# A hybrid decoder step on one core: three gate projections of the first chunk are split, their second halves moved behind the second tile's mixing

## The reference, cut to what matters

```
h = rmsnorm(x)
u_s5, x_lru, y_lru, g_a, g_b = split(h @ w_in)         # 512, 512, 512, 1024, 1024 columns
a_out = s5_branch(u_s5)                                # diagonal state space, then a gated product (w_glu)
b_out = rglru_branch(x_lru, y_lru)                     # convolution, gated scan
merged = sigmoid(g_a) * (a_out @ w_proj_a) + sigmoid(g_b) * (b_out @ w_proj_b)
x = x + merged @ w_out
q = rmsnorm(x) @ w_q                                   # 8 heads, 2 x 128 columns each
x = x + peer(...)     # per token and head: the 16 best of 128 x 128 experts; each gives a row of u and one of v
y = rmsnorm(x)
```

## Time and profile before

| | us |
|---|---|
| median of 3 runs | 3078.5 |
| lowest, highest | 3077.85, 3082.4 |
| profiled execution, its own time | 3078.11 |
| its span in the trace | 3075.9 |
| first gather issued | 188.71 |
| gather 8 issued | 210.43 |

### The profile page before, as it was taken

How to read it: one execution, slowest core, us unless ns; L and a number is a source line. 1 busy time by engine, 2 the same in 40 slices (tenths; PEclk the granted TensorE clock), 3 DMA queues, 4 the chain that set the end, 5 groups by cost and what they waited for, 6 DMA issues and landing times.

```text
span 3075.9 us, 40789 instructions
## 1 busy us (share of the span) xinstructions
PE 2371.8 (77%) x14580; PEld 1201.6 (39%) x14580; DVE 2151.1 (70%) x5362; ACT 1001.8 (33%) x3275; POOL 1201.1 (39%) x1048
## 2 busy tenths in 40 slices
PE   9997768889877778888877768888987775555565
PEld 8864325555343334454333324445433331111111
DVE  7758887765579887665468987766558887554445
ACT  2224433422234332432234332432233433222223
POOL 0014443333334444333343443334344344445443
PEclk9998989999988888989988879999989897777778
DMA  4569999999999999999999999999999999999998
GB/s 154 205 244 394 420 421 420 415 410 414 419 420 419 420 418 405 421 413 420 420 418 416 420 421 407 420 392 420 419 418 421 405 420 420 421 420 421 416 421 336
DMA packets 177354, 1224.74 MB, mean 398 GB/s; under 512 B 22504, under 2 KB 22888, under 8 KB 31616
## 3 DMA queue, kind: packets, MB, share of 16 engines
q0 software_dynamic: 148608, 1082.20, 85.1%
q1 hardware_dynamic: 27040, 135.62, 11.1%
q10 hardware_dynamic: 1504, 4.33, 0.4%
HBM read 1217.55 MB, written 4.51 MB: 397 GB/s over the span
## 4 chain that ended last, share of the span: by engine, by line
DMA 43%; PE 29%; DVE 15%; ACT 4%; POOL 4%; issue 3%; ACTq 1%; DVEq 0%; POOLq 0%
DMA arena<-in_uv,arena 42%; PE psum L2128 12%; PE psum L2022 8%; DVE arena L1702 7%; POOL arena L749 4%; ACT arena L797 4%; PE psum L2172 3%; DVE arena L1200 3%; PE psum L2192 2%; DVE arena L1208 1%; DMA arena<-in_w_ab 1%; PE psum L2204 1%; PE psum L2037 1%; ACT L797 1%; PE psum L2061 1%
## 5 line engine op out<-in xcount | busy, mean ns | idle before, releaser
L749 POOL DMA_INDIRECT arena<-in_uv,arena x1032 | 1197.9, 1161 | 1848.1 <-PE psum L2128 1505.5
L1702 DVE CUSTOM_DVE_ANT_0 arena<-arena 128x1024 f32<-128x1024 f32 x1024 | 1246.9, 1225 | 787.1 <-DMA arena<-in_uv,arena 752.2
L2128 PE MATMUL psum<-arena 64*64 64x512 f32 x8184 | 1214.2, 717 | 652.6 <-ACT arena L797 597.9
L797 ACT ACTIVATE arena<-arena 128x1 f32<-128x1 f32 (+4 forms) x2746 | 726.9, 302 | 1827.6 <-DVE arena L1702 1685.3
L2128 PEld LDWEIGHTS psum<-arena 64*64 64x64 f32 x8184 | 302.5, 151 | 1374.0 <-ACT arena L797 885.1
L2022 PE MATMUL psum<-arena 128*128 128x256 f32 (+1 forms) x2656 | 637.9, 396 | 8.6 <-ACT arena L797 6.1
L2022 PEld LDWEIGHTS psum<-arena 128*128 128x128 f32 x2656 | 508.0, 196 | 193.5 <-issue 118.4
L1200 DVE TENSOR_TENSOR arena<-arena 128x256 f32<-128x256 f32 (+12 forms) x561 | 250.0, 472 | 12.1 <-issue 0.4
L797 ACT ACT_TABLE_LOAD x119 | 152.7, 1283 | 11.1 <-DVE arena L1200 7.0
L797 ACT ACTIVATE arena<-psum 128x256 f32<-128x256 f32 (+5 forms) x254 | 98.6, 403 | 159.5 <-PE psum L2022 108.0
L2172 PE MATMUL psum<-arena 128*128 128x128 f32 (+2 forms) x640 | 120.7, 346 | 9.5 <-DMA arena<-in_w_ab 7.3
(11 more groups left out here) (137 smaller groups left out, 1000.4 us busy)
## 6 DMA issues: line engine op xcount, KB each, us to landing
arena<-in_w_in SPq DMA_DIRECT2D x56, 1024.0 KB
arena<-in_w_q SPq DMA_DIRECT2D x34, 1024.0 KB
arena<-in_uv,arena POOLq DMA_INDIRECT x1032
arena<-in_w_ab SPq DMA_DIRECT2D x12, 1024.0 KB
arena<-in_w_out SPq DMA_DIRECT2D x11, 512.0 KB, 16.0
arena<-in_keys SPq DMA_DIRECT2D x17, 256.0 KB, 15.1
arena<-in_w_ab SPq DMA_DIRECT2D x8, 512.0 KB, 11.1
arena<-in_x_tok SPq DMA_DIRECT2D x8, 512.0 KB
```

The source lines that it names most:

```text
L749: pool.indirect_dma_start(uvring[:, r], None, i_["uv"], bass.IndirectOffsetOnAxis(column, 0)).then_inc(uv_in[r], 16)
L797: return nc.scalar.activation(out, in_, f, **kw)
L1702: V.tensor_tensor_reduce(out=u, in0=u, in1=hn[i // (SLOT // 2)], scale=1.0, scalar=0.0, op0=ALU.mult, op1=ALU.add, accum_out=dots_[:, b % ...
L2128: ins = mm(PV[o:o + HP, half], dg[r:r + HP, PAIR * (b % 2) + k], uvring[r:r + HP, place(c, i) % UV, at:at + 512], start=(i % (SLOT // 2) = ...
```

## The change

For the first chunk the projections of slots 25, 26 and 27 (`LATE`; `m` = 13, 14, 15) take columns 0 to 127 only, and so does their tanh. Their columns 128 to 255 are projected after the second tile's mixing and before `head(1)`, as three units of their own (`U_LATE`), with a tanh each on ScalarE. Since `hT[0]` must live until then, the second tile's mixing writes to `ga`. The columns of `w_in` for `g_b` are reordered on the host (`GB_OF`), so that the three late blocks are `m` = 3, 4, 5, which the second mixing takes last. The weights stay: block 25 gets a home in `hn[1]` and a load of its own, 26 and 27 remain in their place of the ring. All counts of `unit` and `evac` behind move by three.

```diff
-U_MIX0, U_OUT0, U_Q0, U_MIX1, U_Q01, U_OUT1, U_Q1, UNITS0 = 36, 44, 52, 54, 62, 64, 72, 88
-SLOTS0 = UNITS0 - 4
+U_MIX0, U_OUT0, U_Q0, U_MIX1, U_LATE, U_Q01, U_OUT1, U_Q1, UNITS0 = 36, 44, 52, 54, 62, 65, 67, 75, 91
+GB_OF = (0, 1, 2, 6, 7, 3, 4, 5)
+LATE, LATE_FROM = (25, 26, 27), 20
+SLOTS0 = UNITS0 - 4 - len(LATE)
...
-HOMES = RESIDENT + PARKED + GLU_W + tuple(MIX_W)
+HOMES = RESIDENT + PARKED + GLU_W + tuple(MIX_W) + (("w_in", LATE[0]),)
...
 def slot_unit(c, l):
-    return l if l < U_GATE else ga_unit(c, l - U_GATE) if l < TRUNK else l + (8 if c else 4)
+    if c == 0 and l in LATE:
+        return U_LATE + l - LATE[0]
+    if l < TRUNK:
+        return l if l < U_GATE else ga_unit(c, l - U_GATE)
+    return l + (8 if c else 4 if l < U_Q01 - 4 - len(LATE) else 4 + len(LATE))
...
# ScalarE, before the queries of head 1
+                        for j, l in enumerate(LATE):
+                            act.wait_ge(unit, U_LATE + j + 1)
+                            af(gb[:, GB_OF[l - LATE_FROM], P:C], PB[j % 2][:, 0:P], ACT.Tanh, scale=0.5).then_inc(evac, 1)
...
# VectorE, second mixing
+                    held = [GB_OF[l - LATE_FROM] for l in LATE]
+                    if m in held:
+                        dve.wait_ge(evac, U_MIX0 + 2 + held.index(m) + 1)
-                    mix(0, m, U_MIX1 + 4 * (i // 4) + 3, late, [...])
+                    mix(0, m, U_MIX1 + 4 * (i // 4) + 3, late, [...], ga)
...
# TensorE, behind the second mixing
                 pe.wait_ge(hn_ok, 1)
+                for j, l in enumerate(LATE):
+                    w = slot(0, l)
+                    if j >= 2:
+                        pe.wait_ge(evac, U_MIX0 + 2 + j - 1)
+                    for t in range(KT):
+                        ins = mm(PB[j % 2][:, 0:P], w[:, P * t:P * t + P], hT[0][:, t, late], start=(t == 0), stop=(t == KT - 1))
+                    ins.then_inc(unit, 1)
                 head(1, U_Q01)
...
-                    project(c, ga_unit(c, m), U_GATE + m, hT[c], KT, n)
+                    project(c, ga_unit(c, m), U_GATE + m, hT[c], KT, P if first and U_GATE + m in LATE else n)
```

More of the change, by code:

```diff
@@ L64 @@
 EVACS = 56
-U_MIX0, U_OUT0, U_Q0, U_MIX1, U_Q01, U_OUT1, U_Q1, UNITS0 = 36, 44, 52, 54, 62, 64, 72, 88
-SLOTS0 = UNITS0 - 4
+U_MIX0, U_OUT0, U_Q0, U_MIX1, U_LATE, U_Q01, U_OUT1, U_Q1, UNITS0 = 36, 44, 52, 54, 62, 65, 67, 75, 91
+GB_OF = (0, 1, 2, 6, 7, 3, 4, 5)
+LATE, LATE_FROM = (25, 26, 27), 20
+SLOTS0 = UNITS0 - 4 - len(LATE)
 TRUNK = 28
-EVACS0 = 56
+EVACS0 = 56 + len(LATE)
 LAST_FIRST = (6, 7, 0, 1, 2, 3, 4, 5)
@@ L469, in build @@
             + [rows_[:, GLU_AT + DB * k:GLU_AT + DB * k + DB] for k in range(QT)] \
-            + [rows_[:, MIX_AT + D * k:MIX_AT + D * k + D] for k in (LAST_FIRST.index(m) for m in range(KT))]
+            + [rows_[:, MIX_AT + D * k:MIX_AT + D * k + D] for k in (LAST_FIRST.index(m) for m in range(KT))] \
+            + [hn[1]]
         dg = R.take(2 * PAIR, HP)
@@ L1066, in mixing_gate @@
                     act.wait_ge(unit, units(c) + u + 1)
-                    dst = (ga if m < KT else gb)[:, m % KT, 0:n]
+                    w = P if first and U_GATE + m in LATE else n
+                    dst = ga[:, m, 0:w] if m < KT else gb[:, GB_OF[m - KT], 0:w]
                     if m == KT:
                         act.wait_ge(halo_ok, c + 2)
-                    af(dst, PB[u % 2][:, 0:n], ACT.Tanh, scale=0.5).then_inc(evac, 1)
+                    af(dst, PB[u % 2][:, 0:w], ACT.Tanh, scale=0.5).then_inc(evac, 1)
                 for q in range(QT):
@@ L1779, in sample_scale, with mix @@
                 stt(x_tok[0:NS, 1], x_tok[0:NS, 1], ss[0:NS, 1:2], nfs[0:NS], ALU.mult, ALU.mult).then_inc(yos_ok, 1)
-            def mix(c, m, u, cols, bank):
+            def mix(c, m, u, cols, bank, mixed):
                 dve.wait_ge(unit, u + 1)
@@ L1787, in mix @@
                 settled(stt(B2, B2, 1.0, bank[1][:, 0:n], ALU.add, ALU.mult))
-                stt(hT[c][:, m, cols], A, 0.5, B2, ALU.mult, ALU.add).then_inc(mix_ok, 1)
+                stt(mixed[:, m, cols], A, 0.5, B2, ALU.mult, ALU.add).then_inc(mix_ok, 1)
             def residual_half(t, rn, banks, half):
@@ L1832, in first_lists @@
                 for m in range(KT):
-                    mix(0, m, U_MIX0 + m, early, MIXB[m % 2])
+                    mix(0, m, U_MIX0 + m, early, MIXB[m % 2], hT[0])
                 dve.wait_ge(tok_in, 32)
@@ L1857, in first_lists @@
                         upto(OLD + 1)
-                    mix(0, m, U_MIX1 + 4 * (i // 4) + 3, late, [b[:, P * (i % 4):P * (i % 4) + P] for b in MIXB[i // 4]])
+                    held = [GB_OF[l - LATE_FROM] for l in LATE]
+                    if m in held:
+                        dve.wait_ge(evac, U_MIX0 + 2 + held.index(m) + 1)
+                    mix(0, m, U_MIX1 + 4 * (i // 4) + 3, late, [b[:, P * (i % 4):P * (i % 4) + P] for b in MIXB[i // 4]], ga)
                 dve.wait_ge(s_ev, 2)
@@ L1929, in chunk @@
                     upto(at_mix(m) + 1)
-                    mix(c, m, units(c) + U_MIX + m, slice(0, n), MIXB[m % 2])
+                    mix(c, m, units(c) + U_MIX + m, slice(0, n), MIXB[m % 2], hT[c])
                 upto(AT_X2)
@@ L2198, in query @@
                 def query(u, s, cols, evicted):
-                    w = slot(0, u - 4)
+                    w = slot(0, u - 4 - (len(LATE) if u >= U_Q01 else 0))
                     pe.wait_ge(evac, evicted)
@@ L2257, in head @@
                 def head(h, first_unit):
+                    passed = U_MIX0 + (2 + len(LATE)) * h
                     for s in range(2):
-                        query(first_unit + s, s, early, U_MIX0 + 2 * h)
-                    pe.wait_ge(evac, U_MIX0 + 2 * h + 2)
+                        query(first_unit + s, s, early, passed)
+                    pe.wait_ge(evac, passed + 2)
                     for s in range(2):
@@ L2283, in first_lists @@
                     pe.wait_ge(mix_ok, KT + i + 1)
-                    w = slot(0, U_OUT1 - 4 + k)
+                    w = slot(0, U_OUT1 - 4 - len(LATE) + k)
                     for half in range(2):
-                        ins = mm(PB[half], hT[0][:, k, late], w[:, 512 * half:512 * half + 512], start=(i == 0), stop=(i == KT - 1))
+                        ins = mm(PB[half], ga[:, k, late], w[:, 512 * half:512 * half + 512], start=(i == 0), stop=(i == KT - 1))
                     ins.then_inc(unit, 1)
@@ L2296, in first_lists @@
                 pe.wait_ge(s_ev, 2)
+                passed = U_MIX0 + len(LATE)
                 for h in range(2, HEADS):
@@ L2299, in first_lists @@
                         upto(at0_proj(h, s))
-                        query(U_Q1 + 2 * (h - 2) + s, s, slice(0, C), U_MIX0 + 2 * h + s - 1)
+                        query(U_Q1 + 2 * (h - 2) + s, s, slice(0, C), passed + 2 * h + s - 1)
                     upto(at0_scores(h))
-                    pe.wait_ge(evac, U_MIX0 + 2 * h + 2)
+                    pe.wait_ge(evac, passed + 2 * h + 2)
                     pe.wait_ge(key_in[h // 2 % 2], 16 * ((h // 2 - 1) // 2 + 1))
@@ L2315, in first_lists @@
                         upto(at0_proj(HEADS, 0) + 2 * h + s)
-                        query(U_Q1 + 12 + 2 * h + s, s, late, U_MIX0 + 16 + 2 * h + s - 1)
+                        query(U_Q1 + 12 + 2 * h + s, s, late, passed + 16 + 2 * h + s - 1)
                 upto(at0_scores(HEADS))
@@ L2492 @@
     w_in = tiles(a["w_in"][0])
+    w_in[LATE_FROM:] = w_in[[LATE_FROM + m for m in GB_OF]]
     gate = np.stack([a["lru_w_a"][0], a["lru_w_x"][0]])
```

## The result

| | before | after |
|---|---|---|
| median of 6 runs, us | 3080.28 | 3094.23 |
| lowest, highest | 3077.85, 3082.4 | 3091.17, 3095.36 |
| profiled execution, its own time | 3078.11 | 3091.17 |
| span in the trace | 3075.9 | 3088.9 |

The ratio is 1.0047, with a 95% interval of 1.0037 to 1.0056: the change costs 13.95 us by the medians, 13.06 us between the two profiled executions. The forecast was 3091.5 us, with a range of 3084 to 3097, against a median before of 3078.5; as a shift it was +13.3 us.

The account below looks back on a forecast made before the run. Up to about 250 us the gather stream was taken to hang on TensorE's order, so delaying `head(1)` delays it: -3.65 + 5.5 + 9.0 + 2.5 = +13.3 us on 3078.1, forecast 3091.5 us, range 3084 to 3097.

Parts of the forecast that it names:

- Part 1: Front, three shortened projections: gain 3.65 us, not 5.5, as TensorE waits for VectorE's last scan piece; 140 to 189 us shifts whole.
- Part 2: Late halves on TensorE between the second mixing and `head(1)`: three times 1.83 us, +5.5 us; their tanh cost nothing.
- Part 3: Load of head 1's query weights, held by SyncE until the third late projection is done; `head(1)` waits for it: +9.0 us.
- Part 4: Clock falls to half while TensorE idles for the load, slowing `head(1)`: +2.5 us, bounds 0 and 2.7.
- A: Rival: the load of head 1's weights is the bound but dearer, 13 us; 3095.6 us; chance 0.16.
- B: Rival: the load of head 1's weights is cheaper, 5.5 us, with no clock term; 3085.5 us; chance 0.16.
- C: Rival: no wait before `head(1)`, the load isn't held; only 1.85 us of TensorE remain; 3080.0 us; chance 0.06.
- D: Rival: gather stream bound by its start and bytes, not `head(1)`; -3.65 and +2.4 us, 3076.9 us; chance 0.06.
- E: Rival: as D, with part 1's whole 5.5 us and without 1.0 us of DMA idle at 240 to 243; 3071.6; chance 0.04.

Follow-up runs that it names:

- e2: Changed kernel, with head 1's two query weight blocks given places of their own and loaded before 180 us; 3081.36 against 3078.70 us for the kernel before, ratio 1.0009.
- e1: Kernel before, with only one added wait: SyncE holds the load of head 1's query weights until the second mixing's eighth unit; 3091.71 against 3078.70 us, ratio 1.0040.
- e8: Kernel before, with SyncE holding the load of head 1's query weights only until the first tile's output product is through; 3079.66 against 3079.14 us, ratio 1.0002.
- e4: Changed kernel, with 22 unread products on TensorE ahead of head 1's queries; 3090.91 against 3078.70 us for the kernel before, ratio 1.0039.
- e7: Kernel before, with eight unread products in TensorE's gap before the `values` at 237.31 us; 3076.46 against 3079.14 us, ratio 0.9993.

## Why the prediction was right, step by step

The mechanism, its place and the end were as forecast; that the sum came so close is partly luck. The terms, at gather 8, from the rows above:

| term | forecast | measured |
|---|---|---|
| front, until gather 0 | -3.65 | -3.34 |
| late halves, to 202.48 | +5.5 | +5.5 |
| load of head 1's weights | +9.0 | +10.1 |
| half clock in the queries | +2.5 | +2.3 |
| sum at gather 8 | +13.3 | +14.66 |
| at the end (profiled executions) | +13.3 | +13.06 |

**Part 1** held, the wait for VectorE too. It was mis-sized by 0.3 us. TensorE resumed at 133.61 where I had 133.5, and the third projection became shorter by 1.68 us, not 1.85: from its start to that of the gated product are 1.88 us (134.61 to 136.49), before 3.56 (136.28 to 139.84). The length of the first two doesn't count, since TensorE waits behind them. The chain from 140 to 189 us shifted whole; the weights were no limit.

**Part 2** held. I put the tanh behind the projections at nothing; e2 shows that the last of them holds the queries for 0.46 us. In the changed kernel that is hidden under the load.

**Part 3** was the deciding term, and e1, e2 and e8 show it alone, removed, and harmless. It was undersized by 1.1 us. The wait for the first packet was 3.4 us, near my 3, and SyncE's queue got rather more than half of the engines; but I counted 1 MB for it, and it moved 1.71 MB until the load had landed. I had looked for loads ahead of this one in its queue and had cost those behind it, the keys and the next pair, at nothing. In e1, where the gathers had more left to move, the queue had moved 1.12 MB from its first packet to 209.5 us, and the load took 9.2 us. What the load would have taken with nothing behind it wasn't tried. What it takes without gathers is shown by e8: 4.7 us, against 10.1. The estimate by the Trainium skill (DMA: Bandwidth & Descriptors, Anatomy of one DMA), 4.4 us, is near e8's 4.7, but less than half of what the load took here, where the first packet alone took 3.4 us.

**Part 4** held, and e4 shows that it is the clock and not the memory: 6.05 against 3.84 us with TensorE kept busy. That its size came within 0.2 us is luck: the clock was back 4.7 us after work resumed, in e1 2.8 us after, at a cost of 1.4. The Trainium skill (TensorE: Matmul & The Clock Gate, HAM oscillation) says that products behind such a wait for a DMA start at the slow clock, and the granted clock of 0.50 behind the wait of 10.16 us agrees.

**The sum** was right in part by offsetting errors: 1.4 us too little at gather 8 (the terms leave 0.1 us of rounding and semaphores). At the end 1.6 us were given back. About 1 us of that shows behind the next gap, where the clock came back sooner than before: the `values` took 3.34 and the queries behind them 3.72 us, in the kernel before 3.69 and 4.44.

```profile
255.25 3.72 PE L2218 MATMUL psum<-arena 128*128 128x256 f32 x16
```

This need not be the change's doing: in e8, which alters nothing near this gap, they took 3.50 and 3.82 us. The rest isn't pinned down; the profiled executions are single ones, and the runs of one kernel differ by some 4 us.

The rivals: A and B had the right mechanism at other prices; the load at 10.1 us lay between the forecast and A. C would have needed e1 to be free. D and E stand on a stream that isn't bound by `head(1)`; the engines did run dry, from 214 us on (forecast 212), for 8.8 us (forecast 11), before gather 8 came. Two sums of the prediction are off: E leaves out the +2.4 us that D has, with which it is 3074.0, and the new start of the output product is 158.72 - 3.65 = 155.1 us, not 155.2. Neither changes the forecast.

## What to carry to other kernels

Work that is moved takes its operands' places with it. Before moving a product, ask which buffer its weights hold until then, which load waits for that buffer, and what comes right behind the product in its engine's order; here the moved 5.5 us of TensorE cost 2.7, net of the 3.2 gained at the front (e2), and the weights that waited for their place cost 11. A load on demand under a stream of gathers should be priced by a load that the trace shows under the same stream, not by bytes over bandwidth; what is issued right behind it in its own queue counts too, and the half clock behind the wait belongs to its price. And work that must be moved is free only in a wait that is there already: look for the waits of its engine between its earliest and its latest place, and cut no more off the front than the other engine's chain lets one have.

## What the runs showed of the hardware

A load of 1 MB from SyncE, issued while the gathers fill the engines, moved its first packet 3.3 to 3.4 us after the issue and landed after 9.0 us (before), 9.2 (e1) and 10.1 us (changed kernel); the load of the next chunk's columns in the changed kernel, at 242.9 us, took 6.9. With the engines idle (e8) the first packet came 0.9 us after the issue, and the last had moved after 4.7. By the granted shares of short stretches of the traces, the clock fell 1.9 us after TensorE had stopped in the kernel before (233.7 to 235.6 us), 4.6 us after in the changed kernel (202.5 to 207.1 us) and 5.2 in e1 (200.3 to 205.5). Once work had resumed it was back after 5.1 us in the kernel before and 4.7 in the changed one, but after 2.8 in e1 and 2.9 at the later gap of the changed kernel, from 251.97 us. Products that nobody reads, in the place of the wait, kept it at 1.00 each time (e4, e7).
